# Order of the w_pg loads and of the gate units in the piece stage of a fused encoder layer

## What is computed

```python
h = h + hier_moe(rmsnorm(h, g_moe), w_rg, b_rg, w_re, b_re, w1, w3, w2)
pe = rmsnorm(p @ w_ple, g_ple)
gate = sigmoid(rmsnorm(h, g_pg) @ w_pg + b_pg)
h = h + gate * pe
```

## Time and profile before

| what | value |
|---|---|
| median of 3 runs | 1387.44 us |
| the profiled execution, its own time | 1388.14 us |
| its span, first to last instruction | 1386.1 us |
| mean granted TensorE clock | 0.900 of full speed |
| TensorE (PE) busy | 1089.3 us, 79% |
| VectorE (DVE) busy | 285.3 us, 21% |
| ScalarE (ACT) busy | 156.7 us, 11% |
| read from HBM | 473.12 MB |

### The profile page before, as it was taken

One profiled execution on the slowest core, in us unless ns is written; L12 is line 12 of the kernel. 1 busy time (PEld: TensorE's weight loads), 2 busy tenths in 40 slices (PEclk: granted clock), 3 DMA queues, 4 the chain that ended last, 5 costly groups with the idle time before them and its releaser, 6 DMA issues.

```text
span 1386.1 us, 13825 instructions
## 1 busy us (share of the span) xinstructions
PE 1089.3 (79%) x6016; PEld 504.8 (36%) x6016; DVE 285.3 (21%) x439; ACT 156.7 (11%) x314; POOL 53.4 (4%) x66
## 2 busy tenths in 40 slices
PE   8999999999876686666765667666576656989998
PEld 4458887445522232222222223222232212333333
DVE  1104726412321212121221121000000000111116
ACT  1111315002200011000000000000000000010102
POOL 0112110200000002000000000000000000000000
PEclk9999999999888899788898788888888877999999
DMA  9943334354599999999999999999999999999961
GB/s 351 305 152 122 122 122 147 129 217 182 227 426 426 429 426 427 429 426 428 429 426 428 428 426 426 415 427 428 414 427 415 427 428 409 384 395 387 397 267 61
DMA packets 91053, 476.14 MB, mean 344 GB/s; under 512 B 10272, under 2 KB 10416, under 8 KB 67952
## 3 DMA queue, kind: packets, MB, share of 16 engines
q1 hardware_dynamic: 84896, 471.88, 84.1%
q0 software_dynamic: 560, 2.88, 0.6%
q10 hardware_dynamic: 5536, 0.47, 0.3%
HBM read 473.12 MB, written 2.10 MB: 343 GB/s over the span
## 4 chain that ended last, share of the span: by engine, by line
DMA 50%; PE 47%; SPq 1%; DVE 1%; issue 1%; ACT 0%; DVEq 0%
DMA ring<-in_w 48%; PE ps L1421 8%; PE ps L1384 6%; PE ps L1851 6%; PE ps L1674 5%; PE ps L1754 4%; PE ps L1545 4%; PE ps L1558 4%; PE ps L1809 2%; DMA area<-in_w 2%; PE ps L1646 2%; PE ps L1822 1%; PE ps L1639 1%; SPq L386 1%; PE ps L1578 1%
## 5 line engine op out<-in xcount | busy, mean ns | idle before, releaser
L1754 PE MATMUL ps<-ring,area 128*32 128x512 f32 x1024 | 166.4, 796 | 122.6 <-DMA ring<-in_w 122.0
L1674 PE MATMUL ps<-ring,area 128*32 128x512 f32 x976 | 147.7, 724 | 126.2 <-DMA ring<-in_w 126.2
L1184 DVE TENSOR_TENSOR h<-ps,h 128x2048 f32<-128x2048 f32 x32 | 73.3, 2292 | 298.8 <-PE ps L1646 298.8
L1754 PEld LDWEIGHTS ps<-ring,area 128*32 128x32 f32 x1024 | 43.1, 139 | 232.3 <-issue 232.3
L1421 PE MATMUL ps<-hT,ring 128*128 128x256 f32 x512 | 112.9, 380 | 0.0
L1674 PEld LDWEIGHTS ps<-ring,area 128*32 128x32 f32 x976 | 31.6, 122 | 222.7 <-issue 222.4
L1421 PEld LDWEIGHTS ps<-hT,ring 128*128 128x128 f32 x512 | 96.5, 190 | 14.0 <-issue 1.2
L1851 PE MATMUL ps<-ring,area 128*128 128x512 f32 x192 | 88.6, 603 | 6.3 <-DMA ring<-in_w_pg 4.9
L1384 PE MATMUL ps<-ring,hT 128*128 128x512 f32 x192 | 85.0, 602 | 1.1 <-DVE hT L907 1.1
L1229 DVE TENSOR_TENSOR hT<-area,ps 128x128 f32<-128x128 f32 x16 | 4.6, 288 | 315.8 <-ACT area L860 315.8
L1639 PE MATMUL ps<-area,hs 128*128 128x128 f32 x512 | 66.2, 284 | 0.5 <-DVE area L1165 0.5
(11 more groups left out here) (278 smaller groups left out, 775.0 us busy)
## 6 DMA issues: line engine op xcount, KB each, us to landing
ring<-in_w SPq DMA_DIRECT2D x157, 2048.0 KB, 21.5
ring<-in_w SPq DMA_DIRECT2D x57, 1024.0 KB, 15.1
ring<-in_w_in SPq DMA_DIRECT2D x28, 1024.0 KB, 12.6
ring<-in_w_out SPq DMA_DIRECT2D x16, 1024.0 KB, 7.2
ring<-in_w_pg SPq DMA_DIRECT2D x12, 1024.0 KB, 15.7
area<-in_w SPq DMA_DIRECT2D x2, 2048.0 KB, 14.0
hs<-in_w SPq DMA_DIRECT2D x4, 1024.0 KB, 14.3
hs<-in_w_pg SPq DMA_DIRECT2D x3, 1024.0 KB, 17.4
```

Source lines behind the costliest of these rows:

```text
L1184: dve.tensor_tensor(h[:, t, :], ps[:, bank:bank + 4, :].rearrange("p b n -> p (b n)"), h[:, t, :], ALU.add).then_inc(acc_done, 1)
L1674: ins = mm(ps[SLOTS * g:SLOTS * g + SLOTS, 0, :], XG[:, b, k, SLOTS * e:SLOTS * e + SLOTS], s[:, D_EXP * kk:D_EXP * kk + D_EXP], start=(k ...
L1754: ins = mm(ps[SLOTS * g:SLOTS * g + SLOTS, 0, :], XG[:, b, k, SLOTS * e:SLOTS * e + SLOTS], s[:, D_EXP * kk:D_EXP * kk + D_EXP], start=(k ...
```

## The change

It touches pieces 2 and 3. Their w_pg tiles are loaded ahead of the piece's w2 tiles, directly behind the w2 tiles of the piece before. On TensorE every w2 step has two gate units in front of it (the last quad one), and unit 7 stands behind the last scatter; this is the order that piece 1 has already. The places follow from the order of the loads.

```diff
@@ piece_loads
         w_pg_ = [("w_pg", i - 1, kk, 0) for kk in range(4)]
-        order += w_pg_ + w2_ if i == 1 else w2_[:4] + w_pg_ + w2_[4:]
+        order += w_pg_ + w2_
     return order + [("w_pg", PIECES - 1, kk, 0) for kk in range(4)]
@@ TensorE's program
             for i in range(1, PIECES):
                 for q in range(OPEN_QUADS):
-                    if i > 1:
-                        w2_piece(i, q)
-                        if q:
-                            scatter_piece(i, q - 1)
                     gate_unit(i - 1, 2 * q)
                     if q < OPEN_QUADS - 1:
                         gate_unit(i - 1, 2 * q + 1)
-                    if i == 1:
-                        w2_piece(i, q)
-                        if q:
-                            scatter_piece(i, q - 1)
+                    w2_piece(i, q)
+                    if q:
+                        scatter_piece(i, q - 1)
                 scatter_piece(i, OPEN_QUADS - 1)
                 gate_unit(i - 1, 7)
                 turn_piece(i)
```

## The result

| | before | changed |
|---|---|---|
| median, runs side by side | 1386.99 us (5 runs, 1385.63 to 1387.69) | 1380.26 us (5 runs, 1379.44 to 1380.46) |
| the profiled execution, its own time | 1388.14 us | 1380.46 us |
| its span | 1386.1 us | 1378.6 us |
| from the start of the last turn to the end of the span | 36.14 us | 36.15 us |

The ratio is 0.9941, 95% interval 0.9927 to 0.9954: the change is faster by 0.5 to 0.7%, which is 6.4 to 10.1 us. A second set of runs gave 0.9948 (0.9933 to 0.9963). The two medians of the table alone have the ratio 0.9951, 6.7 us.

The account below looks back on a forecast made before the run. TensorE work behind its last wait for a load, at 1312.21, bounds the kernel. Two units (6.87) plus the slow stretch (1.65) less a new wait (0.35) save 8.1: 1380.0 us profiled, 1379.3 median, range 1378.3 to 1382.5.

Parts of the forecast that it names:

- What bounds the kernel: Last 200 us: transfers and TensorE run nearly level; TensorE work behind its last wait for a load, at 1312.21, decides.
- Landings by rank: Loads of the piece stage, numbered 0 to 63 in issue order, keep landing times: 51 at 1312.2, 63 at 1343.7.
- The walk: Step-by-step TensorE timing through pieces 2 and 3: turn at 1341.8, last gate units from 1343.9 instead of 1352.02, saving 8.1 us.
- Idle behind each turn: Between a turn's start and gate unit 0, about 1.1 us of TensorE idle exposed, no w2 step covering hT copies.
- The slow stretch: TensorE steps behind the wait at 1312.21, partly at 1.2 GHz before, would run at full clock, saving 1.65 us.
- two units (6.87): Two gate units of piece 2 move ahead of the last wait at 1312.21, saving 6.87 us.
- The tail of 34.1 us: The last eight gate units hang on the last turn alone and stay at 34.1 us.
- Rival 1: Half-clock stretches of 1.65 us behind the waits at 1312.2, 1333.8 and 1343.9; 3.5 us gained, 1383.9 median; chance 0.10.
- Rival 2: Stream 0.7 us a load slower between loads 51 and 63; gain gone, 1387 us; chance 0.04.
- Rival 3: Places run out in SP's load queue, dry for 10 us, delaying later landings and the end: 1389.3 us; chance 0.03.

## Why the prediction was right, point by point

- **What bounds the kernel.** Right. The stream is as full after as before, the last load lands at the same place in it, and the gain is work of TensorE that moved in front of load 51. The halves run alone show it from both sides: with the loads' order or TensorE's order alone, the last gate units begin 49.0 us behind the wait for load 47, with both 42.5, and with one half alone the time is that of before.
- **Landings by rank.** Right. From load 19 to the wait for load 27 it is 20.7 us in the trace after (1228.12 to 1248.85) for a forecast of 20.8, to that for load 47 it is 73.9 for 74.0.
- **The walk.** Right to a few tenths. From load 19's row: turn of piece 3 at 114.3 us for 114.4, last gate units 116.4 for 116.5. The waits of about 1.1 us stood where the walk had them, with 0.9.
- **Idle behind each turn.** 1.02 us three times, forecast 1.1.
- **The slow stretch (1.65 us of the 8.1).** This is the weak term of the sum. "They consist of two units (6.87), plus the half-clock stretch behind 1312.21": in the trace I read, it was there, and it is gone after. The second trace of before has the same waits and no such stretch. As a difference of two traces 8.1 was right: from load 19's row to the last gate units it is 124.6 us before and 116.4 after, 8.2 less (the profiled executions differ by 7.7, since the stage itself stands 0.7 later). As a forecast for the median, the term had to be weighed by how often it occurs, which one trace can't tell. The medians' 6.7 us stand near the 6.5 without it; the ratio allows both. 1380.26 lies 1.0 above the forecast and inside the range. Counted from the median of before beside which it ran, 1386.99 and not 1387.44, the miss is 1.4; so part of the closeness is luck.
- **The tail of 34.1 us.** Right: 34.10.
- **Rival 1, a slow stretch behind each wait.** Did not come: granted clock 1.00 in pieces 2 and 3. The Trainium skill (TensorE: Matmul & The Clock Gate, "HAM oscillation — how this bites in real kernels") tells of a kernel that waits about 3 to 5 us for each new tile and comes back at the slow clock every time; the prediction left out how long those waits were. The traces here agree with it for the longest waits (TensorE's order alone: 4.33 us of idle at 1243.10, granted clock 0.50 from 1244 to 1248). Shorter waits that follow one another brought the slow clock too, though not always: w_pg's waits in piece 2 in both traces of before (0.60 and 0.53 from 1248 to 1252), the pair in front of load 51 in one of the two. Single waits of 0.9 or 1.0 us with full work around them never did, nor did one of 1.74 us (the run with a wait per block, at 1302.43; granted clock 1.00 from 1300 to 1308).
- **Rival 2, given back to the stream.** Did not come: 0.3 us at load 59, as priced.
- **Rival 3, places.** Did not come, and was farther off than I made it: I counted 8 of 15 places bound and took the edge for near, but 10 places are enough.

## What to carry to other kernels

Where two resources run nearly level, count the work of the one that stands behind the last landing of the other: an order is worth what it takes out of that stretch, and what it wins ahead of an earlier wait is lost at the next one. The order of the loads and the order of their use must then move together. Before a slow-clock stretch of one trace is entered as a gain, take a second trace.

## What the runs showed of the hardware

The clock: the same two waits (0.9 and 1.6 us, TensorE 1.7 to 1.8 us busy of 4) were followed by a stretch at 1.2 GHz in one execution of the kernel before and by full clock (2.4 GHz) in another. I had taken it for a property of the kernel. In piece 2 of the kernel before, where four waits of 0.4 to 1.5 us follow one another, both traces have a slow stretch, but it begins one wait earlier in the second (the step at 1245.75 takes 2.07 us there, the one at 1245.65 took 1.13). It cost nothing, since the wait for load 31 behind it took it in.

The queue: 10 places were enough to keep it full in pieces 2 and 3. How far ahead of its landing SP issues a load (14.5 us in the median with 15 places) is not what the transfer needs: with 8 places loads landed 5.4 us behind their issue at the shortest, and only there did the stream show gaps in pieces 2 and 3.
